# mLSTM output gates and values as one product in seven quarters, its weight sums on GpSimd

## The reference

```python
proj = x @ w_in
aq, ak, av, mq, mk, mv, mo, mi, mf = jnp.split(proj, offs, axis=-1)
hm = mlstm_chunkwise(mq, mk, mv, ...)          # 4 heads of 128
hm = layernorm_per_head(hm) * mlstm_norm_w
hm = jax.nn.sigmoid(mo) * hm
```

## Time and profile before

| what | value |
|---|---|
| median of three runs | 1160.19 us |
| the profiled execution's own time | 1160.38 us |
| its span, first to last instruction | 1158.4 us |
| TensorE busy | 1070.6 us (92%) |
| VectorE busy | 378.1 us (33%) |
| ScalarE busy | 168.5 us (15%) |
| GpSimd busy | 64.8 us (6%) |
| DMA, mean over the span | 384 GB/s |
| mean granted TensorE clock | 0.965 of full speed |

### The profile page before, as it was taken

The page is one execution under the profiler, slowest core; times in us unless marked ns, Lnnn a source line. Parts: engine busy times, 40 slices in busy tenths (PEclk is TensorE's granted clock), DMA queues, the critical chain, the costliest instruction groups (busy, mean ns, idle before and its releaser), DMA issues.

```text
span 1158.4 us, 20097 instructions
## 1 busy us (share of the span) xinstructions
PE 1070.6 (92%) x8036; PEld 469.1 (40%) x8037; DVE 378.1 (33%) x1230; ACT 168.5 (15%) x380; POOL 64.8 (6%) x40
## 2 busy tenths in 40 slices
PE   9999999998999669999976669999989989998997
PEld 8668649653333213333322223333323333332333
DVE  1716545254333113333311113333323313332323
ACT  1123211211111001111100001111111111111112
POOL 0520451000000000000000000000000000000000
PEclk9999999999999979999998889999998999999999
DMA  9984246959999999999999999999999999999996
GB/s 329 374 287 146 74 145 255 409 198 411 427 435 432 431 431 431 429 434 432 432 431 431 433 429 434 432 431 432 430 432 431 433 430 428 432 429 432 430 423 250
DMA packets 36670, 445.33 MB, mean 384 GB/s; under 512 B 3936, under 2 KB 5216, under 8 KB 21696
## 3 DMA queue, kind: packets, MB, share of 16 engines
q1 hardware_dynamic: 33888, 439.85, 90.3%
q10 hardware_dynamic: 2752, 5.04, 1.3%
HBM read 443.84 MB, written 1.05 MB: 384 GB/s over the span
## 4 chain that ended last, share of the span: by engine, by line
PE 72%; DMA 23%; another core or an unknown queue 2%; DVE 2%; ACT 1%; issue 0%; SPq 0%; DVEq 0%
PE bank L923 23%; PE bank L948 13%; DMA ring<-in_w_down 11%; DMA ring<-in_w_gu 11%; PE bank L899 6%; PE bank L600 6%; PE bank L617 5%; PE bank L886 3%; PE bank L819 2%; PE bank L756 2%; PE bank L698 2%; PE bank L892 1%; PE bank L930 1%; PE bank L936 1%; PE bank L941 1%
## 5 line engine op out<-in xcount | busy, mean ns | idle before, releaser
L923 PE MATMUL bank<-ring,wk 128*32 128x512 f32 x3072 | 371.1, 634 | 64.7 <-DMA ring<-in_w_gu 64.7
L923 PEld LDWEIGHTS bank<-ring,wk 128*32 128x32 f32 x3072 | 103.9, 116 | 304.2 <-issue 266.4
L948 PE MATMUL bank<-ring,wk 128*32 128x512 f32 x1632 | 205.5, 601 | 7.4 <-DMA ring<-in_w_down 7.3
L1829 DVE TENSOR_SCALAR wk<-bank 128x256 f32<-128x256 f32 x51 | 21.6, 424 | 536.1 <-PE bank L923 536.1
L899 PE MATMUL bank<-wk 64*128 64x512 f32 x416 | 103.3, 615 | 2.9 <-ACT wk L1329 2.9
L948 PEld LDWEIGHTS bank<-ring,wk 128*32 128x32 f32 x1632 | 63.4, 110 | 76.9 <-issue 48.9
L1315 ACT ACTIVATE wk<-wk 128x256 f32<-128x256 f32 x51 | 21.2, 416 | 455.2 <-DVE wk L1829 455.2
L600 PE MATMUL bank<-ring 128*128 128x256 f32 x320 | 70.4, 380 | 0.0
L899 PEld LDWEIGHTS bank<-wk 64*128 64x128 f32 x416 | 35.8, 186 | 71.5 <-issue 64.1
L600 PEld LDWEIGHTS bank<-ring 128*128 128x128 f32 x320 | 60.3, 190 | 8.4 <-issue 0.3
L886 PE MATMUL bank<-res,wk 128*32 128x256 f32 x832 | 56.5, 389 | 0.0
(11 more groups left out here) (333 smaller groups left out, 860.7 us busy)
## 6 DMA issues: line engine op xcount, KB each, us to landing
ring<-in_w_gu SPq DMA_DIRECT2D x55, 4096.0 KB, 34.7
ring<-in_w_down SPq DMA_DIRECT2D x27, 4096.0 KB, 38.3
ring<-in_w_gu SPq DMA_DIRECT2D x18, 2048.0 KB, 14.5
ring<-in_w_down SPq DMA_DIRECT2D x9, 2048.0 KB, 11.9
ring<-in_w_in SPq DMA_DIRECT2D x4, 2048.0 KB, 24.5
ring<-in_w_ck SPq DMA_DIRECT2D x2, 2048.0 KB, 22.0
ring<-in_w_cv SPq DMA_DIRECT2D x2, 2048.0 KB, 13.8
ring<-in_w_out SPq DMA_DIRECT2D x2, 2048.0 KB, 15.2
```

The costliest lines, as they stand in the source:

```text
L923: ins = mm(hidden(bank, g), rows[:, kk, c, :], half_columns(w[:, kk, :], g), start=False, stop=2 * c + kk == KT - 1, skip_group_check=True)
L948: ins = mm(strip(7, 2 * d + b), actT[:, b, 2 * c + gg, :], wd[:, gg, b, 512 * d:512 * d + 512], start=c == 0 and gg == 0 and b == 1, stop= ...
```

## The change

The two projections "mo" and "mv" become one: x by the two weight blocks side by side is a product of 2x2 quarters (two token tiles, two halves of the 1024 inputs, two column blocks mo and mv), computed with seven quarter products of four 128x128 by 128x512 each, in place of eight. Four sums of x's quarters (`mo_s1` to `mo_s4`) are made on VectorE, ahead of all its other work, and four of the weights' quarters (`mo_t1` to `mo_t4`, 128x2048 each) on GpSimd, ahead of the bias splitting. mo_t1 lives in the buffer of x's rows (`res`), mo_t2 in `wk`, mo_t3 and mo_t4 in place. Products accumulate in banks 2, 3 and 0. ScalarE copies partial results out between them and VectorE adds them, so that gates and values share their common parts. ScalarE loads the sigmoid table once more and the exponentials' table again. The load of x's rows and of the first norm's rows are issued later on ScalarE's queue, the load of memT one piece later on SyncE's. "aq" now uses banks 2 and 3.

```diff
@@ UNITS and slots
-        UNITS = ["akav", "mq", "mk", "mo", "mv", "aq", "ck0", ...
+        UNITS = ["akav", "mq", "mk", "aq", "ck0", ...
+            elif piece in ("mo", "mv"):
+                eng.wait_ge(mo_product, 7)
...
@@ SyncE
-                if n == 3:
+                if n == 4:
                     sp.dma_start(memT_sb, ...).then_inc(memT_landed, 16)
@@ GpSimd
             nc.gpsimd.memset(bgu_raw, 0.0).then_inc(zero_done, 1)
+            for nm in ("mo", "mv"):
+                s, n = front_slot(nm)
+                pool.wait_ge(slot_landed[s], 16 * n)
+            nc.gpsimd.tensor_tensor(mo_t1, mo_quarter[0][1], mo_quarter[0][0], ALU.subtract).then_inc(mo_sums, 1)
+            pool.wait_ge(mo_sums, 1)
+            nc.gpsimd.tensor_tensor(mo_t2, mo_quarter[1][1], mo_t1, ALU.subtract).then_inc(mo_sums, 1)
+            nc.gpsimd.tensor_tensor(mo_t3, mo_quarter[1][1], mo_quarter[0][1], ALU.subtract).then_inc(mo_sums, 1)
+            pool.wait_ge(mo_product, 2)
+            pool.wait_ge(mo_sums, 3)
+            nc.gpsimd.tensor_tensor(mo_t4, mo_quarter[1][0], mo_t2, ALU.subtract).then_inc(mo_sums, 1)
             pool.wait_ge(bgu_landed, 48)
             pool.wait_ge(parts_ready, 1)
@@ TensorE
-            project("mo", xk, between=lambda: turn_parts(2))
+            landed("mo")
+            X, Y, Z = psum[2], psum[3], psum[0]
+            wait_taken(pe, "mq")
+            quarter_product(X, x_quarter[0][0], mo_quarter[0][0]).then_inc(mo_product, 1)
+            quarter_product(Y, x_quarter[0][1], mo_quarter[1][0]).then_inc(mo_product, 1)
+            landed("mv")
+            pe.wait_ge(mo_rows, 2)
+            pe.wait_ge(mo_sums, 2)
+            pe.wait_ge(mo_copied, 1)
+            quarter_product(X, mo_s2, mo_t2, fresh=False).then_inc(mo_product, 1)
+            wait_taken(pe, "mk")
+            quarter_product(Z, mo_s1, mo_t1, between=lambda: turn_parts(2)).then_inc(mo_product, 1)
             spread_rows(2)
-            project("mv", xk)
+            pe.wait_ge(mo_sums, 3)
+            pe.wait_ge(mo_copied, 2)
+            quarter_product(X, mo_s3, mo_t3, fresh=False).then_inc(mo_product, 1)
+            pe.wait_ge(mo_copied, 3)
+            quarter_product(Z, mo_s4, mo_quarter[1][1], fresh=False).then_inc(mo_product, 1)
+            pe.wait_ge(mo_sums, 4)
+            pe.wait_ge(mo_added, 2)
+            quarter_product(X, x_quarter[1][1], mo_t4, fresh=False).then_inc(mo_product, 1)
...
+            pe.wait_ge(mo_out, 1)
             project_T("aq", xk)
             pe.wait_ge(wts_ready, 3)
-            wait_taken(pe, "mv")
+            pe.wait_ge(mo_added, 3)
@@ ScalarE
-            act_e.dma_start(res[:], x...).then_inc(x_landed, 16)
...
-            act_e.dma_start(lnp, ln_p[0:1]...).then_inc(ln_landed[0], 16)
             wait_taken(act_e, "mq")
             af(sigq[:, 0:4], mqT, ACT.Sigmoid).then_inc(sig_ready, 1)
+            act_e.wait_ge(mo_product, 1)
+            af(sigo[:, 0, :], psum[2][:], ACT.Copy).then_inc(mo_copied, 1)
             wait_taken(act_e, "mk")
             af(sigq[:, 4:8], mkT, ACT.Sigmoid).then_inc(sig_ready, 1)
-            wait_unit(act_e, "mo")
-            for t in range(TT):
-                af(sigo[:, t, :], unit_banks("mo")[t][:], ACT.Sigmoid).then_inc(taken["mo"], 1)
             nc.scalar.preload_act_table_set(EXP_LN)
+            act_e.wait_ge(mo_product, 3)
+            copy_values(0, psum[2])
+            act_e.wait_ge(mo_product, 4)
+            act_e.dma_start(res[:], x...).then_inc(x_landed, 16)
+            act_e.dma_start(lnp, ln_p[0:1]...).then_inc(ln_landed[0], 16)
+            copy_values(1, psum[0])
             act_e.wait_ge(mask_ready, TT)
...
-            wait_unit(act_e, "mv")
-            ...
+            nc.scalar.preload_act_table(ACT.Sigmoid)
+            act_e.wait_ge(mo_product, 7)
+            af(sigo[:, 1, :], psum[2][:], ACT.Sigmoid).then_inc(mo_out, 1)
+            act_e.wait_ge(mo_added, 1)
+            af(sigo[:, 0, :], sigo[:, 0, :], ACT.Sigmoid).then_inc(mo_out, 1)
+            nc.scalar.preload_act_table_set(EXP_LN)
             act_e.wait_ge(bgu_split, 1)
@@ VectorE
+            for i in range(HEAD):
+                dve.wait_ge(head_landed[i], 32)
+            v.tensor_tensor(mo_s1, x_quarter[1][0], x_quarter[1][1], ALU.add)
+            link(v.tensor_tensor(mo_s3, x_quarter[0][0], x_quarter[1][0], ALU.subtract))
+            v.tensor_tensor(mo_s2, mo_s1, x_quarter[0][0], ALU.subtract).then_inc(mo_rows, 1)
+            dve.wait_ge(mo_rows, 1)
+            v.tensor_tensor(mo_s4, x_quarter[0][1], mo_s2, ALU.subtract).then_inc(mo_rows, 1)
             dve.wait_ge(par_landed, 16)
...
             rows_plus(posm, mask_ready)
-            wait_taken(dve, "mo")
+            dve.wait_ge(mo_product, 2)
+            dve.wait_ge(mo_copied, 1)
+            v.tensor_tensor(sigo[:, 0, :], sigo[:, 0, :], psum[3][:], ALU.add).then_inc(mo_added, 1)
+            dve.wait_ge(mo_product, 5)
+            dve.wait_ge(mo_copied, 3)
+            add_values(1, psum[2])
+            dve.wait_ge(mo_product, 6)
+            dve.wait_ge(mo_copied, 2)
+            add_values(0, psum[0])
+            dve.wait_ge(mo_out, 2)
             for t in range(TT):
                 ins = v.tensor_tensor(sigo[:, t, :], sigo[:, t, :], normw, ALU.mult)
```

More of the change, by code:

```diff
@@ L174, in layer_program @@
         queries = [[cqT[:, 4 - 4 * i:8 - 4 * i, t * P:t * P + P] for i in range(2)] for t in range(TT)]
+        x_quarter = [[xk[:, 4 * h:4 * h + 4, t * P:t * P + P] for h in range(2)] for t in range(TT)]
+        mo_quarter = [[slot_words(front_slot(nm)[0])[:, half * h:half * h + half].rearrange("p (k n) -> p k n", k=KT // 2) for nm in ("mo", "mv")]
+                      for h in range(2)]
+        mo_s1, mo_s2, mo_s3, mo_s4 = (w.rearrange("p (k t) -> p k t", k=KT // 2)
+                                      for w in (wk[:, 2048:2560], wk[:, 2560:3072], qbuf[:, 0:512], qbuf[:, 512:1024]))
+        mo_t1 = res[:].rearrange("p t (k n) -> p (t k) n", n=512)
+        mo_t2 = wk[:, 0:2048].rearrange("p (k n) -> p k n", k=KT // 2)
+        mo_t3, mo_t4 = mo_quarter[0][1], mo_quarter[1][0]
         values = [[memV[:, t, 512 * i:512 * i + 512] for i in range(2)] for t in range(TT)]
@@ L264, in layer_program @@
         mixer_done, sums_ready, values_ready = sem("mixer_done"), sem("sums_ready"), sem("values_ready")
+        mo_product, mo_rows, mo_sums, mo_copied, mo_added, mo_out = (sem("mo_product"), sem("mo_rows"), sem("mo_sums"), sem("mo_copied"),
+                                                                     sem("mo_added"), sem("mo_out"))
         x_landed, memT_landed = sem("x_landed"), sem("memT_landed")
@@ L324, in layer_program @@
         front_loads = [len(range(s, len(PIECES), FRONT_SLOTS)) - (s == 0) if s < FRONT_SLOTS else 0 for s in range(RING)]
-        UNITS = ["akav", "mq", "mk", "mo", "mv", "aq", "ck0", "ck1", "cvA", "hmT", "pv", "wo0", "wo1",
+        UNITS = ["akav", "mq", "mk", "aq", "ck0", "ck1", "cvA", "hmT", "pv", "wo0", "wo1",
                  "cvB0", "cvB1", "cvB2", "x1T0", "x1T1", "cvC", "oT0", "oT1", "co_t0", "co_t1", "x2T0", "x2T1", "logit"]
@@ L604, in project_T, with project @@
                 return ins
-            def project(u, lhs, order=range(KT), late=None, between=None):
+            def project(u, lhs, order=range(KT), late=None):
                 banks = open_unit(u)
@@ L612, in project @@
                     for n, k in enumerate(order):
-                        if between and t == 1 and n == 5:
-                            between()
                         if late and t == 0 and n == KT // 2:
@@ L654, in _, with quarter_product @@
             spread_rows(1)
-            project("mo", xk, between=lambda: turn_parts(2))
-            spread_rows(2)
-            project("mv", xk)
+            def quarter_product(bank, rows, cols, fresh=True, between=None):
+                for k in range(KT // 2):
+                    if between and k == 1:
+                        between()
+                    ins = mm(bank[:], rows[:, k, :], cols[:, k, :], start=fresh and k == 0, stop=k == KT // 2 - 1, skip_group_check=True)
+                return ins
+            landed("mo")
[10 more added lines that the diff above has]
+            quarter_product(Z, mo_s1, mo_t1, between=lambda: turn_parts(2)).then_inc(mo_product, 1)
+            spread_rows(2)
+            pe.wait_ge(mo_sums, 3)
[6 more added lines that the diff above has]
+            quarter_product(X, x_quarter[1][1], mo_t4, fresh=False).then_inc(mo_product, 1)
             pe.wait_ge(qk_ready, 2)
@@ L694, in _ @@
             project_T("ck1", memT_sb)
[L696 to L699, removed]
             cv0, cv1 = landed("cv0"), landed("cv1")
@@ L1169, in _ @@
                 act_e.dma_start(bgu_raw[N_EXP * i:N_EXP * (i + 1), :], b_gu).then_inc(bgu_landed, 16)
-            act_e.dma_start(res[:], x.rearrange("(t p) n -> p t n", p=P)).then_inc(x_landed, 16)
```

(27 more changed lines are left out.)

## The result

The changed kernel took 1170.01 us in the median of four runs (1169.5 to 1171.25), the kernel before 1160.38 us beside it. The ratio is 1.0082, with a 95% interval of 1.0071 to 1.0094. So it is 9.6 us slower: on the side forecast and inside the range, but 4.1 us beyond the forecast of 1165.9. The profiled execution took 1169.5 us.

What follows compares the result with a forecast made beforehand. The experts' weight loads set the pace, issued as TensorE frees ring slots, so TensorE's start moves the end. Terms -3.4 + 6.5 + 2.5 + 0.1 = +5.7 us on 1160.19 gave 1165.9 us, range 1156.5 to 1177.5.

Steps and rivals of the forecast that it cites:

- What it removes: TensorE's mo and mv products: 28 products instead of 32, at 0.86 us each, so -3.4 us.
- One for one: Any shift of TensorE's start, told at the aq product, moves the experts' loads and the end by the same amount.
- The landing: Load of mv's weights: lands at 39.6 us instead of 48.0, and GpSimd's first weight sum can start then.
- The cover: Early added work on VectorE, ScalarE and SyncE is hidden behind existing waits or slack and costs nothing.
- the bounds: TensorE's third quarter waiting for GpSimd's second sum: no wait if mv lands at 38.5 us, 0.5 us if at 41.
- The turn, +6.5 us: At turn_parts(2) TensorE waits for VectorE's second split, out at 60.25 us instead of 53.17: +6.5 us.
- the first rival: VectorE's copies and casts also wait for GpSimd; split out at 72.6 us, aq 16.1 late, total 1176.3 us; chance 0.28.
- the sign I had set for it: In the profile after, VectorE's L1430, L1432 and L1434 growing beyond 0.17 us would show that copies and casts lock too.
- The spreading, +2.5 us: At spread_rows(2) TensorE waits for row products ending at 65.6 us, as fm waits for the 4.07 us bias step: +2.5.
- The clock, nothing: TensorE's granted clock: a gap of 6 us could cost up to 1.4 us, but none was taken.
- The last quarter, +0.1 us: TensorE's seventh quarter waits for VectorE's sum that frees bank 2, at 73.1 us, just when wanted: +0.1 us.
- The second rival's point of decision: No collision if the split is out by 53.7 us at turn_parts(2): saving stands, 1156.8 us; chance 0.25.

Runs made afterwards that it cites:

- e2_bias_late: Changed kernel with only GpSimd's bias splitting held back until the masked rows are made: 1164.42 us, ratio 1.0030 to the kernel before.
- e7_keep_busy: Changed kernel with 40 needless 128x128 products on TensorE in the wait before the second turn of the parts: 1171.17 us, ratio 1.0089.
- e9_memT_first: Changed kernel with fourth weight sum and bias splitting held back, and memT's load put back ahead of mv's: 1160.81 us, ratio 1.0010.
- e1_sum4_late: Changed kernel with GpSimd's fourth weight sum, and all behind it, held back until the second split's rows are placed: 1157.94 us, ratio 0.9970.
- e4_before_bias_shifted: Kernel before, with only GpSimd's bias splitting started later, when the second sigmoid is done: 1172.66 us, ratio 1.0095.
- e8_pieces: Changed kernel with bias splitting held back and each weight sum cut in four GpSimd instructions of 512 columns: 1164.98 us, ratio 1.0037.

## Why the prediction was right, and where it was off

**What it removes** was right: 3.44 us less, seen bare in the run with the first sum on VectorE.

**One for one** was right as far as the router. From the start of "aq" to the router's first product of 128x512 it is 179.71 to 179.76 us in all the eleven profiled executions, with "aq" anywhere from 70.89 to 87.76 us. What I missed lies behind it: that product and its neighbours ran at full rate in eight executions and at the lower clock in the other three (the kernel before, with a granted clock of 0.53 from 253.4 to 257 us, `e2_bias_late`, `e7_keep_busy`), as in these timelines of TensorE, first of the kernel before, then after.

```profile
253.47 1.95 PE L861 MATMUL bank<-ring,late_c 128*128 128x512 f32 x2
255.21 1.91 PE L864 MATMUL bank<-res,wk 128*128 128x512 f32 x2
```

```profile
264.11 1.10 PE L903 MATMUL bank<-ring,late_c 128*128 128x512 f32 x2
265.05 1.02 PE L906 MATMUL bank<-res,wk 128*128 128x512 f32 x2
```

From there to the experts' first product it was 7.35 us before and 5.86 after. So of +10.63 at "aq" (9.57 and 1.06 of the start) +9.15 reached the experts, and +9.2 the span. That the whole came out near the block's own 9.57 is in part chance: 1.06 of the start and -1.49 at the router nearly cancel. From the experts' first product to the end it is 897.5 to 897.7 us in eight executions, but 898.4 in `e9_memT_first`, 899.2 in `e7_keep_busy` and 901.1 in `e1_sum4_late`, whose profiled execution was the slowest of its ten (1160.9 us); what adds there is open. Both blur differences of a few us between single executions, so the gains are told by the medians.

**The landing** was right: 39.6 forecast, 40.2 measured (issue at 14.9, 25.3 us to landing), with sums of 4.5 us. The cover of ScalarE's, SyncE's and VectorE's early work held; no wait of TensorE in the block ends on them. A slip in the bounds changes nothing: two sums after a landing at 41 end at 50.1, so the third quarter would wait 0.8 us, not 0.5.

**The turn, +6.5 us**, is the term that was mis-sized: it measured +9.99. I let only two-input instructions wait and so had the cast L1488 (L1430 before) pass. It was held for the whole fourth sum (4.41 us), and the next sum, which I had passing at its end, met the first bias cast (1.79), the second the long bias step (3.90). The casts wait, as in the first rival; by the sign I had set for it (L1430 longer too) its rule is right and mine wrong. But its 1176.3 us is 6.3 too high: it let one VectorE instruction through per GpSimd instruction, and it is two where GpSimd's are linked by a wait. Its recorded sum also has a slip: the split out at 72.6 gives 15.5 us, not 16.1.

**The spreading, +2.5 us**, was wrong: no wait. I had fm held by the 4.07 us bias step, but that step had already held L1491, and fm met only a cast (1.86). The rows were ready at 67.7 us, and at full clock TensorE would have come at 67.8 (an estimate: 65.05 and the 2.8 us of six records). In the run with TensorE kept busy, at full clock, there is no wait either.

**The clock, nothing**, was wrong too. I had bounded it at 1.4 us by a stretch with 3.4 us of idle time and taken none; in the block it was 3.0, and the run with TensorE kept busy shows that it cost nothing beyond the waits of VectorE, as the last quarter would have waited instead.

**The last quarter, +0.1 us**, came out at no wait: the sum out of its bank ended at 77.93, the quarter was due at 78.2. Only with the clock restored does it wait, 2.6 us. The parts of the sum were not independent, and the three errors (+3.5, -2.5, +3.0) leave 4 us. That they partly cancel is luck. The sign is not: TensorE came to wait at the place forecast, for the cause forecast. That the time lies in the range says little, as the range was 21 us wide and held gains too.

**The second rival's point of decision**, the turn at 53.7, was the right one: the four versions that have the split out by 55.5 us are faster than before, the others (57.9 us and later) are not.

## What to carry to other kernels

Before work is put on GpSimd, list what VectorE does in the same stretch and who waits for it: a chain of eight tiny SBUF instructions on the critical path lost a whole GpSimd instruction at every one or two of them here. Order GpSimd's long instructions around such chains with waits; cutting them in four did not help here. And where a saving of 3 us on TensorE rests on a wait of VectorE, measure that wait first: one line of synchronisation here decided between 9.6 us lost and 3 us gained.

## What the runs showed of the hardware

- VectorE instructions of eight columns with a single source in SBUF (cast, tensor by a constant) wait for a GpSimd instruction to its end: 4.41 us (changed kernel), 3.97 and 3.92 (`e4_before_bias_shifted`) and 4.43 (`e9_memT_first`) instead of 0.17. Those that read PSUM did not: L1497 took 1.27 us beside the bias splitting, as before. But the GpSimd cast that began 0.1 us after it (L536) took 2.88 us where it took 1.89 before, and what held it is not shown.
- Between two GpSimd instructions linked by a wait two VectorE instructions got through, between two that are not linked one (changed kernel, `e8_pieces`).
- GpSimd waits too: 5.44 us for 4.5 behind a q/k product (`e1_sum4_late`).
- TensorE's clock: after 9.93 us of idle time six records took 5.49 us for 2.84 (granted clock 0.51), after 10.22 us 4.91, after 4.74 us 4.29, after 4.04 us 4.54. After a wait of 3.00 us eight took 5.37 for 3.60. After 2.61, 1.69 and 0.84 us they ran at full rate. At the router it fell without idle time just before it: TensorE was busy 4.40 of 4.40 us up to 253.4 us in the kernel before, and the granted clock behind that was 0.53; in the changed kernel it was 1.00 there.
